# First pass on a 512-column ramp: three strips begin with four row tiles, both K strips take six of the later ten first, the other scale and shift columns come in between

## The chip, the cores and the metric

The kernel runs on 1 core of a Trainium2 chip. Its time is the device time of that core in microseconds; the kernel before is given as the median of three runs. TensorE (PE) has a clock that the chip grants at one of two levels, 1.2 or 2.4 GHz; the profile prints the granted share.

## The reference

One decoder layer in float32 on 256 tokens of width 2048: an mLSTM mixer and a gated MLP with a causal convolution, each behind an RMS norm that is modulated by a conditioning vector `c`.

```python
def modulation(c, w_mod, b_mod):
    m = jax.nn.silu(c) @ w_mod + b_mod
    return jnp.split(m[:, None, :], 6, axis=-1)
...
        sh1, sc1, g1, sh2, sc2, g2 = modulation(c, *mod_params[layer])
        hm = rms_norm(x) * (1.0 + sc1) + sh1
        if layer % N_MIXERS == 0:
            y = mlstm_mixer(hm, l0_w_in, l0_gate_bias, l0_h_norm, l0_w_out)
...
        x = x + g1 * y
        hf = rms_norm(x) * (1.0 + sc2) + sh2
        x = x + g2 * conv_ffn(hf, *ffn_params[layer])
```

`mlstm_mixer` begins with `proj = h @ w_in`, whose 6144 wide columns are the queries, keys (K), values (V) and output gates (O), and 16 small gate columns. The change touches only the first modulation (`sc1`, `sh1`: each 2048 columns of `w_mod`, 16.8 MB) and the product `h @ w_in`.

## The kernel before

**Staging of the product.** The product is cut into 12 strips of 512 columns (four V, four O, two K, two Q) and the 2048 rows of `w_in` into 16 row tiles of 128. A unit of work is a half: two row tiles of one strip, 512 KB, 12 matmuls of 512 columns. A half arrives in one of eight places of `raw`; ScalarE (ACT) rounds it to `w_hi` (`split_hi`), VectorE (DVE) makes the rest `w_lo` (`split_lo`, one 128x1024 subtract, counted by `raw_done`), and PE multiplies both with the modulated tokens `hm_hi`, `hm_lo`. `w_hi` and `w_lo` have four places. DVE's and ACT's loops over `p` split half `p + 3` while PE works on half `p`; ACT first waits until PE has done `p` halves. In the text p is the number of a half in PE's order and half v is the same count for loads.

**Two passes.** The first pass (p = 0 to 35) takes the first six row tiles of all 12 strips, three halves each. The second pass (p from 36, `V_PASS1`) takes the other ten row tiles, five halves each, the K strips first. A strip's partial sums lie in two PSUM banks; ACT stores them when the strip is done (`store_strip`) and puts them back for the second pass.

**Why two passes.** A row tile of tokens can be modulated only when its 128 columns of scale and shift are known, and each of those is a sum over all 2048 rows of `w_mod`. The first 768 columns come first: 16 loads `m0` of 768 KB, added on DVE (`add_m0`) and summed on PE (`sum_m0`, `add_first_sums`, with `keep_clock` matmuls between). This stretch is the ramp; PE's first half follows it. The other 1280 columns are added while PE works on the first pass: 32 loads `m1` of 640 KB with one 128x1280 add each (`add_m1`). Their sums are turned by PE (`later_sums`, `turn_rows`), copied by ACT, and the last ten row tiles are modulated at the border of the passes.

**The order of loads.** SyncE (SP) issues all these loads in one order written out by hand, one `m1` load ahead of each half:

```python
            for i in range(2 * KT - 2):
                load_m1(i)
                load_half(6 + i)
...
                    sp.wait_ge(m1_used, i - 5)
...
                    sp.wait_ge(raw_done, RAW0 + vh - 8 + 1)
```

So half v is issued when half v - 8 has been split and the `m1` load before it has its place, one of six. SP waits at an issue that has no place yet, and everything behind it in the order waits too. After the first modulation, 48 loads of 1 MB (`load_mod`, `MOD_LOAD`, `MOD_SLOT`) bring the gate and the second modulation during the second pass and the output projection.

Of the kernel before, what the change touches and what calls it, by code (L numbers as in the profile page):

```python
# [5 lines left out]
def hybrid_mlstm_convffn_adaln_kernel(nc, x_d, c_d, w_mod, b_mod, w_in, gate_bias, h_norm, w_out,  # L6
# [3 lines left out]
    ALU = mybir.AluOpType  # L10
# [57 lines left out]
    M0_COLS, M1_COLS = K_FIRST * P, (KT - K_FIRST) * P  # L68
    WIDE = (85, 128)
# [3 lines left out]
    MOD_SLOT = [V_PASS1 + p for p in (5, 7, 8, 10, 12, 13, 15, 17, 18)] \  # L73
# [11 lines left out]
    MOD_LOAD = [V_PASS1 + 5, V_PASS1 + 6] + [max(V_PASS1 + 6, p + 11) for p in MOD_SLOT[:K_THREE]] \  # L85
# [8 lines left out]
    GROUP = 3 * P  # L94

    GATES_AT = [V_PASS1 + 7 + n for n in range(KT // 2)]
    ROW_KB = (96, 97, 98, 99, 100, 102, 111, 112)
    KQ_TURN = [PAIRS[1] * (s + 1) + 1 for s in range(4)]
    KQ_COPY = [r + 2 for r in KQ_TURN]

    with ExitStack() as ctx:
# [6 lines left out]
        def place(name, shape, offset, dt=f32):  # L108
# [7 lines left out]
        m1 = [place(f"m1_{s}", [P, M1_COLS], (104 if s < 3 else 32) * KB + 4 * M1_COLS * (s % 3))  # L116
              for s in range(6)]
# [63 lines left out]
        sum_rows = [first_rows, first_rows, place("sc2_rows", [P, QUARTER], 189 * KB)]  # L181
# [34 lines left out]
        m1_in = [sem(f"m1_in{s}") for s in range(6)]  # L216
# [151 lines left out]
        def _(sp):  # L368
# [47 lines left out]

            def load_m1(i):
# [7 lines left out]
                col = MOD_ORDER[n] + M0_COLS  # L425
                sp.dma_start(m1[i % 6][:], w_mod[rows:rows + P, col:col + M1_COLS])\
                  .then_inc(m1_in[i % 6], 16)

            def load_half(vh):
# [3 lines left out]
                if vh < 8:  # L433
                    wait_m0((8, 9, 9, 10, 11, 11, 12, 13)[vh])
# [30 lines left out]
            for i in range(2 * KT - 2, 2 * KT):  # L465
                load_m1(i)
            for i in range(2 * KT - 2, 2 * KT):
                load_half(6 + i)
            for vh in range(6 + 2 * KT, V_OUT):
# [65 lines left out]
        def _(pool):  # L535
# [29 lines left out]
            pool.wait_ge(colsum_done, 3)  # L565
            clear_acc(2)
            pool.wait_ge(colsum_done, 4)
            clear_acc(3)
            pool.dma_start(wg_raw[:], w_in[:, COL_G:COL_G + 2 * H].rearrange("(k p) n -> p k n", p=P))\
                .then_inc(wg_in, 16)  # L570
            pool.wait_ge(wg_in, 16)
            for n in range(4):
                for j in range(2):
# [5 lines left out]
                    nc.gpsimd.tensor_tensor(lo, src, hi.bitcast(f32), ALU.subtract).then_inc(wg_made, 1)  # L579

# [58 lines left out]
            pool.wait_ge(colsum_done, 5)  # L639
# [24 lines left out]
        def _(act):  # L664
# [58 lines left out]


# [112 lines left out]
            scale_shift(0, 1, first_sums(0), scale_p[:, 0:K_FIRST], True)  # L837
# [3 lines left out]
            act.wait_ge(xT_copied, K_FIRST // 2)  # L841
            for g in range(K_FIRST // 2):
                modulate_hi(0, 2 * g, 2 * g + 2)
                if g == 0:
                    scale_shift(1, 2, first_sums(1), shift_p[:, 2:K_FIRST], False)
                    act.wait_ge(sc_made, 2)
                if g < 2:
                    split_hi(g + 1)
            act.wait_ge(xT_copied, KT // 2)

            for p in range(V_PASS1):
                wait_from_1(act, half_done, p)
# [1111 lines left out]
```

## Time and profile before

| | |
|---|---|
| median of three runs | 1175.02 us (1174.92 to 1175.26) |
| profiled execution, its own time | 1175.44 us |
| its span | 1173.7 us (1.7 us less than its time) |
| PE busy | 1155.1 us, 98% of the span |
| DVE / ACT / GpSimd busy | 917.8 / 625.8 / 167.7 us |
| first half begins | 44.14 us |
| second pass begins | 146.34 us |

The busy shares are averages over stages. The change lies in the first 175 us: the ramp, where PE waits for loads, and the first pass, where PE hardly pauses. Each row of the trace has a start and a duration in microseconds, the engine, the line, output and inputs, and in brackets how long the engine was idle before it and what released it.

### The profile page before, as it was taken

How to read it: one execution, taken by the hardware profiler on the slowest of the kernel's cores; microseconds unless marked ns; L12 is line 12 of the kernel's file. 1: busy time of each engine (PE TensorE's matmuls, PEld its weight loads, DVE VectorE, ACT ScalarE, POOL GpSimd, SP SyncE). 2: the span in 40 equal slices, each digit the busy share in tenths (PEclk: the TensorE clock that was granted, in tenths of full speed). 3: DMA queues.
4: the chain of work that ended last, by engine and by line, in shares of the span. 5: the costliest groups of instructions: out<-in, count | busy, mean ns of one | idle time of the engine just before them, and what ended most of it. 6: DMA issues, size and time to landing. Idle time of an engine off the chain costs nothing.

```text
span 1173.7 us, 17088 instructions
## 1 busy us (share of the span) xinstructions
PE 1155.1 (98%) x5888; PEld 980.9 (84%) x5888; DVE 917.8 (78%) x998; ACT 625.8 (53%) x911; POOL 167.7 (14%) x171
## 2 busy tenths in 40 slices
PE   5999999999999999999999999999999999999998
PEld 5888788888887888888888888888888788888886
DVE  6899897998989979888885547888885446777766
ACT  4444565666554556555554446555554445555442
POOL 0000140202121321222120001122120001221200
PEclk9999999999999999999999999999999999999999
DMA  9999999999999967988867577788775666666562
GB/s 371 397 401 402 398 364 346 368 406 376 367 383 369 399 184 209 258 222 257 235 217 244 183 230 232 209 260 233 210 235 197 219 194 185 194 193 179 195 197 74
DMA packets 260953, 316.66 MB, mean 270 GB/s; under 512 B 6328, under 2 KB 187264, under 8 KB 251944
## 3 DMA queue, kind: packets, MB, share of 16 engines
q1 hardware_dynamic: 259488, 312.50, 80.0%
q0 software_dynamic: 944, 3.34, 0.8%
q8 instruction: 28, 0.46, 0.2%
q10 hardware_dynamic: 474, 0.21, 0.1%
q14 instruction: 19, 0.16, 0.0%
HBM read 313.90 MB, written 2.12 MB: 269 GB/s over the span
## 4 chain that ended last, share of the span: by engine, by line
PE 95%; DMA 3%; DVE 1%; SPq 1%; POOL 0%; ACT 0%; issue 0%; DVEq 0%
PE ps L1497 27%; PE ps L1503 14%; PE ps L1537 9%; PE ps L1539 9%; PE ps L1538 9%; PE ps L1608 7%; PE ps L1609 7%; PE ps L1611 7%; DMA m<-in_l_w_mod_dram 3%; PE ps L1616 1%; SPq L413 0%; PE ps L1643 0%; POOL small L593 0%; PE ps L1776 0%; PE ps L1733 0%; PE ps L1826 0%
## 5 line engine op out<-in xcount | busy, mean ns | idle before, releaser
L1116 DVE TENSOR_TENSOR w_lo<-raw,w_hi 128x1024 fp32r<-128x1024 f32 x384 | 471.4, 1230 | 156.5 <-ACT w_hi L676 155.4
L676 ACT ACTIVATE w_hi<-raw 128x1024 fp32r<-128x1024 f32 x384 | 406.0, 1058 | 346.6 <-PE ps L1539 152.0
L1497 PE MATMUL ps<-hm,w_hi 128*128 128x512 f32 x1406 | 338.9, 391 | 0.2 <-DVE hm L1401 0.2
L1497 PEld LDWEIGHTS ps<-hm,w_hi 128*128 128x128 f32 x1406 | 257.4, 188 | 49.0 <-DVE hm L1401 0.4
L1503 PEld LDWEIGHTS ps<-hm,w_lo 128*128 128x128 f32 x1408 | 182.7, 191 | 8.2
L1503 PE MATMUL ps<-hm,w_lo 128*128 128x256 f32 x1408 | 185.3, 283 | 0.0
L1608 PE MATMUL ps<-w_hi,hm 128*128 128x512 f32 x380 | 151.9, 400 | 0.4 <-ACT hm L720 0.4
L1609 PE MATMUL ps<-w_lo,hm 128*128 128x512 f32 x380 | 148.3, 390 | 0.0
L1611 PE MATMUL ps<-w_hi,hm 128*128 128x512 f32 x352 | 137.5, 391 | 0.0
L1537 PE MATMUL ps<-w_hi,act_hi 128*128 128x512 f32 x344 | 134.1, 390 | 0.0
L1538 PE MATMUL ps<-w_lo,act_hi 128*128 128x512 f32 x344 | 134.0, 390 | 0.0
L1539 PE MATMUL ps<-w_hi,act_lo 128*128 128x512 f32 x344 | 134.0, 390 | 0.0
L650 POOL TENSOR_TENSOR act_full<-conv_gate,conv_val 128x256 f32<-128x256 f32 x44 | 32.5, 740 | 510.8 <-DVE conv_val L1444 510.8
L1078 ACT ACTIVATE up_sum<-ps 128x256 f32<-128x256 f32 x84 | 32.0, 381 | 106.4 <-PE ps L1497 106.4
L1608 PEld LDWEIGHTS ps<-w_hi,hm 128*128 128x128 f32 x380 | 71.4, 188 | 18.6 <-issue 3.2
L1609 PEld LDWEIGHTS ps<-w_lo,hm 128*128 128x128 f32 x380 | 71.5, 188 | 14.0
L1135 DVE SCALAR_TENSOR_TENSOR acc<-mod_raw,cT,acc 128x2048 f32<-128x2048 f32 x32 | 75.0, 2345 | 6.1 <-DMA mod_raw<-in_l_w_mod_dram 3.5
L1611 PEld LDWEIGHTS ps<-w_hi,hm 128*128 128x128 f32 x352 | 66.1, 188 | 14.2
L1537 PEld LDWEIGHTS ps<-w_hi,act_hi 128*128 128x128 f32 x344 | 64.6, 188 | 14.2 <-issue 0.8
L1539 PEld LDWEIGHTS ps<-w_hi,act_lo 128*128 128x128 f32 x344 | 64.6, 188 | 13.4
L1538 PEld LDWEIGHTS ps<-w_lo,act_hi 128*128 128x128 f32 x344 | 64.6, 188 | 13.3
L654 POOL TENSOR_TENSOR act_lo<-act_full,act_hi 128x256 f32 x44 | 65.4, 1486 | 23.7 <-DVE act_hi L1451 23.7
(199 smaller groups left out, 1114.9 us busy)
## 6 DMA issues: line engine op xcount, KB each, us to landing
raw<-in_l_w_up_dram SPq DMA_DIRECT2D x88, 1024.0 KB, 5.9
raw<-in_l_w_in_dram SPq DMA_DIRECT2D x96, 512.0 KB, 12.2
mod_raw<-in_l_w_mod_dram SPq DMA_DIRECT2D x48, 1024.0 KB, 7.5
raw<-in_l_w_down_dram SPq DMA_DIRECT2D x44, 1024.0 KB, 5.0
m<-in_l_w_mod_dram SPq DMA_DIRECT2D x32, 640.0 KB, 14.3
raw<-in_l_w_out_dram SPq DMA_DIRECT2D x16, 1024.0 KB, 10.2
m<-in_l_w_mod_dram SPq DMA_DIRECT2D x15, 768.0 KB, 13.1
mod_third<-in_l_w_mod_dram SPq DMA_DIRECT2D x8, 1024.0 KB, 8.1
```

The lines of the kernel that those rows point to most:

```text
L654: nc.gpsimd.tensor_tensor(act_lo[:, part], act_full[:, k, :], act_hi[:, part].bitcast(f32), ALU.subtract)\
L676: nc.scalar.activation(w_hi[:, v % 4, :], raw_half(v), ACT.Copy).then_inc(w_hi_made, 1)
L1116: nc.vector.tensor_tensor(w_lo[:, v % 4, :], raw_half(v), w_hi[:, v % 4, :].bitcast(f32), ALU.subtract)\
L1135: nc.vector.scalar_tensor_tensor(out=part, in0=src, scalar=cT[:, ds(tile, 1)], in1=part, op0=ALU.mult, op1=ALU.add).then_inc(mod_done, 1)
L1497: return mm(ps[:, 4 + w % 4, :], w_hi[:, v % 4, j * P:(j + 1) * P], both, start=(k == 0), stop=stop, skip_group_check=True)
L1503: return mm(ps[:, 4 + w % 4, 0:SEQ], w_lo[:, v % 4, j * P:(j + 1) * P], hm_hi[:, k, :], start=False, stop=stop, skip_group_check=True)
L1537: mm(out, s_hi, hi, start=first, stop=False, skip_group_check=True)
L1538: mm(out, s_hi, lo, start=False, stop=False, skip_group_check=True)
L1539: last = mm(out, s_lo, hi, start=False, stop=final, skip_group_check=True)
L1608: mm(out, s_hi, hi, start=(k == 0), stop=False, skip_group_check=True)
L1609: mm(out, s_hi, lo, start=False, stop=False, skip_group_check=True)
L1611: last = mm(out, s_lo, hi, start=False, stop=(k == final), skip_group_check=True)
```

## The change

The ramp's loads are cut to 512 columns of scale and of shift (`M0_COLS`: 16 loads of 512 KB). The first three strips take four row tiles each (p = 0 to 5), then their last two (p = 6 to 8), which need columns 512 to 767: eight new loads `m0b` of 4 x 128 rows by 256 columns, with 32 adds of 256 columns on DVE (`add_m0b`) and the sums `ramp_sums` on PE behind p = 5. The other columns come in two groups: 32 loads of 768 columns and then 32 of 512, in five places in place of six. `m1_due(p)` says how many adds stand behind each split: four to every three halves from p = 6, then three to each half from p = 31 to 41. SP's order follows it: `m1_ahead(vh)` loads are issued before half `vh`. The two K strips of the second pass take row tiles 6 to 11 (p = 36 to 41) and then 12 to 15 (p = 42 to 45). ACT makes the full modulated tile too (`modulate_full`), DVE only subtracts (`low_part`). The loads and adds of the later modulation move three to four halves later.

```diff
-    M0_COLS, M1_COLS = K_FIRST * P, (KT - K_FIRST) * P
-    WIDE = (85, 128)
+    K_RAMP, K_MORE = 4, 12
+    M0_COLS, MB_COLS = K_RAMP * P, (K_FIRST - K_RAMP) * P
+    M1_COLS = ((K_MORE - K_FIRST) * P, (KT - K_MORE) * P)
+    M1_GROUPS = ((3, 2 * P), (4, P))
+    WIDE = (P, P)
+    ORDER = [(m, kp) for m in range(3) for kp in range(2)] + [(m, 2) for m in range(3)] \
+        + [(m, kp) for m in range(3, STRIPS) for kp in range(PAIRS[0])] \
+        + [(STRIPS + m, 3 + kp) for m in range(2) for kp in range(3)] \
+        + [(STRIPS + m, 6 + kp) for m in range(2) for kp in range(2)] \
+        + [(m, kp) for m in range(STRIPS + 2, 2 * STRIPS) for kp in range(3, 8)]
...
-    MOD_LOAD = [V_PASS1 + 5, V_PASS1 + 6] + [max(V_PASS1 + 6, p + 11) for p in MOD_SLOT[:K_THREE]] \
+    MOD_LOAD = [V_PASS1 + 9, V_PASS1 + 9] + [max(V_PASS1 + 9, p + 11) for p in MOD_SLOT[:K_THREE]] \
...
+    ROWS_SUMMED = (18, 31, V_PASS1, V_PASS1 + 5)
+    ROWS_TURNED = (20, 32, V_PASS1 + 2, V_PASS1 + 5)
+    ROWS_COPIED = (19, 32, V_PASS1 + 1, V_PASS1 + 6)
+    SCALES_TAKEN = (21, 33, V_PASS1 + 3, V_PASS1 + 6)
+    MODULATED = (34, 35, V_PASS1, V_PASS1 + 6, V_PASS1 + 7)
...
+        def m1_due(p):
+            if p <= 30:
+                return max(0, min(2 * KT, 4 * (p - 5) // 3))
+            return min(M1_TILES, 2 * KT + 3 * (p - 30))
+
+        def m1_ahead(vh):
+            return min(M1_TILES, m1_due(vh - 5) + 4)
...
+            def load_m0b(i):
+                n, rows = i // 4, 4 * (i % 4) * P
+                if i < 4:
+                    sp.wait_ge(xT_ready, KT // 2)
+                else:
+                    sp.wait_ge(m0b_used, 4 * (i - 3))
...
             def load_m1(i):
-                n, rows = i // KT, (i % KT) * P
-                if i < 3:
+                b, n, rows = i // (2 * KT), i // KT % 2, (i % KT) * P
+                if i < 5:
                     sp.wait_ge(xn_made, TB)
-                elif i < 6:
-                    wait_m0((14, 14, 15)[i - 3])
                 else:
-                    sp.wait_ge(m1_used, i - 5)
+                    sp.wait_ge(m1_used, i - 4)
...
-            for vh in range(6):
+            load_half(0)
+            for vh in range(1, 9):
                 load_half(vh)
-            for i in range(2 * KT - 2):
-                load_m1(i)
-                load_half(6 + i)
+                load_m0b(vh - 1)
+            issued = 0
+            for vh in range(9, V_OUT):
+                while issued < m1_ahead(vh):
+                    load_m1(issued)
+                    issued += 1
                 load_due_mods(vh)
                 load_half(vh)
...
+            def scales_and_shifts(p):
+
+                if p == K_FIRST:
+                    for n, out in ((0, scale_p), (1, shift_p)):
+                        scale_shift(n, 3, ps[:, n, 0:2 * P].rearrange("p (k c) -> p k c", c=P)[:, :, 0],
+                                    out[:, K_RAMP:K_FIRST], n == 0)
+                    act.wait_ge(sc_made, 4)
+                    modulate_hi(0, K_RAMP, K_FIRST)
...
+                if p in MODULATED:
+                    act.wait_ge(sc_made, 6 if p < SCALES_TAKEN[3] else 8)
+                    modulate_later(K_FIRST + 2 * MODULATED.index(p))
...
             for p in range(V_PASS1):
-                if p == V_PASS1 - 1:
-                    dve.wait_ge(sc_made, 6)
-                    modulate_lo(0, K_FIRST, K_FIRST + 2)
+                adds_and_low_parts(p)
                 split_lo(p + 3)
-                if 1 <= p <= 2 * KT:
-                    add_m1(p - 1)
+                for i in range(8):
+                    if (0, 0, 1, 2, 2, 3, 3, 4)[i] == p:
+                        add_m0b(i)
+                for i in range(m1_due(p - 1), m1_due(p)):
+                    add_m1(i)
...
+            def ramp_sums():
+
+                pe.wait_ge(m0b_used, 2 * KT)
+                for n in range(2):
+                    for k in range(2):
+                        c0 = M0_COLS + k * P
+                        last = mm(ps[:, n, k * P:(k + 1) * P], acc[:, n, c0:c0 + P], ones[:], start=True, stop=True)
+                last.then_inc(colsum_done, 1)
```

DVE's order, from the split of half 3 on. Before, a split and one add of 1280 columns take turns (`w_lo` rows are splits, the first pair being those of halves 3 and 4; `acc` rows are adds):

```order
L1116 TENSOR_TENSOR w_lo<-raw,w_hi 128x1024 x2
L1164 SCALAR_TENSOR_TENSOR acc<-m_0_53,cT,acc 128x1280
L1116 TENSOR_TENSOR w_lo<-raw,w_hi 128x1024
L1164 SCALAR_TENSOR_TENSOR acc<-m_1_54,cT,acc 128x1280
L1116 TENSOR_TENSOR w_lo<-raw,w_hi 128x1024
```

In the changed kernel, at the same place (the row ahead of this piece holds the splits of halves 2 and 3; the first split below is that of half 4):

```order
L1215 SCALAR_TENSOR_TENSOR acc<-m0b,cT,acc 128x256 x8
L1165 TENSOR_TENSOR w_lo<-raw,w_hi 128x1024
L1215 SCALAR_TENSOR_TENSOR acc<-m0b,cT,acc 128x256 x4
L1165 TENSOR_TENSOR w_lo<-raw,w_hi 128x1024
L1215 SCALAR_TENSOR_TENSOR acc<-m0b,cT,acc 128x256 x8
L1165 TENSOR_TENSOR w_lo<-raw,w_hi 128x1024
L1215 SCALAR_TENSOR_TENSOR acc<-m0b,cT,acc 128x256 x8
L1165 TENSOR_TENSOR w_lo<-raw,w_hi 128x1024
L1215 SCALAR_TENSOR_TENSOR acc<-m0b,cT,acc 128x256 x4
L1165 TENSOR_TENSOR w_lo<-raw,w_hi 128x1024
L1231 TENSOR_SCALAR hm_full<-hm_full,scale_p,shift_p 128x256
```

The 32 short adds now stand between the splits of halves 3 and 8, and the modulation of row tiles 4 and 5 stands behind them.

SP's order. Before, from the first half on, six halves go first and then one `m` load (1280 columns) and one half in turn:

```order
L439 DMA raw<-in_l_w_in_dram 128x2x512 x6
L426 DMA m_0_53<-in_l_w_mod_dram 128x1280
L439 DMA raw<-in_l_w_in_dram 128x2x512
L426 DMA m_1_54<-in_l_w_mod_dram 128x1280
L439 DMA raw<-in_l_w_in_dram 128x2x512
```

In the changed kernel, behind half 8 and the last `m0b` load:

```order
L460 DMA m_0_53<-in_l_w_mod_dram 128x768
L460 DMA m_1_54<-in_l_w_mod_dram 128x768
L460 DMA m_2_55<-in_l_w_mod_dram 128x768
L460 DMA m_3_56<-in_l_w_mod_dram 128x768
L473 DMA raw<-in_l_w_in_dram 128x2x512 x2
L460 DMA m_4_57<-in_l_w_mod_dram 128x768
L473 DMA raw<-in_l_w_in_dram 128x2x512
L460 DMA m_0_53<-in_l_w_mod_dram 128x768
L473 DMA raw<-in_l_w_in_dram 128x2x512
L460 DMA m_1_54<-in_l_w_mod_dram 128x768
L460 DMA m_2_55<-in_l_w_mod_dram 128x768
L473 DMA raw<-in_l_w_in_dram 128x2x512
```

The last of these is half 13; the `m` load right before it is number 7 (counted from 0), and by `load_m1` it waits for three adds done, the third of which stands behind the split of half 11.

PE's order at the place where the last 512 columns are summed, behind p = 41 (the first two rows end p = 41, the third and fourth are the last sums and their turn):

```order
L1676 MATMUL ps<-w_lo,hm 128x512
L1678 MATMUL ps<-w_hi,hm 128x512
L1710 MATMUL ps<-acc,ones 32x128 x4
L1718 MATMUL ps<-ident,first_rows 128x128
L1675 MATMUL ps<-w_hi,hm 128x512
```

Before, the last such sums stood inside p = 35; they now stand inside the second pass.

## Rows read from the trace of the kernel before

**Rows 1.** The page: chain that ended last, shares of the span by engine

```profile
PE 95%; DMA 3%; DVE 1%; SPq 1%; POOL 0%; ACT 0%; issue 0%; DVEq 0%
```

**Rows 2.** The chain of waits in order of time: start, length, what

```profile
27.25 13.82 DMA m<-in_l_w_mod_dram
```

**Rows 3.** Windows: busy of PE, PEld, DVE, ACT, POOL; granted clock, DMA share, GB/s

```profile
28.00:30.00 2.00, 2.00 (x11) 2.00 (x11) 1.55 (x2) 0.18 (x1) 0.00 (x0) 0.50 1.02 398
30.00:40.00 10.00, 8.89 (x56) 7.74 (x56) 7.24 (x8) 0.00 (x0) 0.00 (x0) 0.96 1.03 399
60.00:80.00 20.00, 20.00 (x90) 16.58 (x89) 19.68 (x16) 9.69 (x12) 0.00 (x0) 1.00 1.04 401
160.00:400.00 240.00, 239.90 (x1111) 197.01 (x1111) 212.75 (x186) 140.21 (x233) 49.93 (x52) 1.00 0.99 375
```

**Rows 4.** Timeline of PE in the ramp, and its first half

```profile
17.54 5.16 PE L1675 MATMUL ps<-ident,xn 128*128 128x128 f32 x32
...
22.54 2.81 PE L1692 MATMUL ps<-c_wide,m 128*128 128x85 f32 x24
...
28.60 2.61 PE L1692 MATMUL ps<-c_wide,m 128*128 128x128 f32 x12
31.04 1.46 PE L1665 MATMUL ps<-still 128*128 128x256 f32 x6
32.34 1.50 PE L1692 MATMUL ps<-c_wide,m 128*128 128x128 f32 x12
...
42.22 1.61 PE L1702 MATMUL ps<-ones,acc 128*128 128x128 f32 x12
...
44.14 1.17 PE L1577 MATMUL ps<-w_hi,hm 128*128 128x512 f32 x4
```

**Rows 5.** Timeline of DVE: first work behind the ramp; split of half 2

```profile
42.97 0.16 DVE L1196 COPY shift_p<-ps 128x2 f32<-128x2 f32 x1 [0.80 <-PE ps L1702]
...
48.51 1.22 DVE L1116 TENSOR_TENSOR w_lo<-raw,w_hi 128x1024 fp32r<-128x1024 f32 x1
```

**Rows 6.** Groups on DVE by shape: busy us, mean ns

```profile
L1164 DVE SCALAR_TENSOR_TENSOR acc<-m,cT,acc 128x1280 f32<-128x1280 f32 x32 | 49.6, 1550 | 5.5 <-DMA m<-in_l_w_mod_dram 5.5
L1155 DVE SCALAR_TENSOR_TENSOR acc<-m,cT,acc 128x768 f32<-128x768 f32 x23 | 23.4, 1018 | 9.7 <-DMA m<-in_l_w_mod_dram 8.7
L1439 DVE SCALAR_TENSOR_TENSOR conv_gate<-up_sum,cvT,conv_gate 128x255 f32<-128x255 f32 x44 | 21.4, 487 | 0.0
```

**Rows 7.** Timeline of DVE in the ramp: three adds in one row

```profile
12.76 3.19 DVE L1155 SCALAR_TENSOR_TENSOR acc<-m,cT,acc 128x768 f32<-128x768 f32 x3 [0.86 <-DMA m<-in_l_w_mod_dram]
```

**Rows 8.** Timeline of PE: start of half 6, of the second pass, around half 43

```profile
60.91 0.39 PE L1608 MATMUL ps<-w_hi,hm 128*128 128x512 f32 x1
...
146.34 0.47 PE L1608 MATMUL ps<-w_hi,hm 128*128 128x512 f32 x1 [0.36 <-ACT hm L720]
...
166.18 1.04 PE L1629 MATMUL ps<-ident,kq 128*128 128x128 f32 x8
166.97 0.48 PE L1608 MATMUL ps<-w_hi,hm 128*128 128x512 f32 x1
...
169.81 0.62 PE L1733 MATMUL ps<-hm,wg 128*104 128x512 f32 x2
170.26 0.39 PE L1608 MATMUL ps<-w_hi,hm 128*128 128x512 f32 x1
```

**Rows 9.** Loads: size each, median us from issue to landing; 0 to 50 us

```profile
raw<-in_l_w_in_dram SPq DMA_DIRECT2D x10, 512.0 KB, 12.3
```

**Rows 10.** The same at the kernel's end, and the DMA's busy tenths there

```profile
DMA  8179049418803793960799920000000053004050
...
raw<-in_l_w_down_dram SPq DMA_DIRECT2D x6, 1024.0 KB, 5.0
```

**Rows 11.** Timeline of ACT at the border of the passes

```profile
145.59 1.09 ACT L720 ACTIVATE hm<-hm_full,shift_p,scale_p 128x256 fp32r<-128x256 f32 x2
146.59 1.04 ACT L676 ACTIVATE w_hi<-raw 128x1024 fp32r<-128x1024 f32 x1
```

More of the change, by code:

```diff
@@ L115, in hybrid_mlstm_convffn_adaln_kernel @@
         m0 = place("m0", [P, 8, 2 * M0_COLS], 0)
-        m1 = [place(f"m1_{s}", [P, M1_COLS], (104 if s < 3 else 32) * KB + 4 * M1_COLS * (s % 3))
-              for s in range(6)]
+        m1 = [place(f"m1_{s}", [P, M1_COLS[0]], 104 * KB + 4 * M1_COLS[0] * s) for s in range(5)]
+        m0b = place("m0b", [P, 4, 4 * MB_COLS], 152 * KB)
         w_hi = place("w_hi", [P, 4, HALF], 48 * KB, f32r)
@@ L215, in hybrid_mlstm_convffn_adaln_kernel @@
         m0_used, m0_summed = sem("m0_used"), sem("m0_summed")
-        m1_in = [sem(f"m1_in{s}") for s in range(6)]
+        m0b_in = [sem(f"m0b_in{s}") for s in range(4)]
+        m0b_used = sem("m0b_used")
+        m1_in = [sem(f"m1_in{s}") for s in range(5)]
         m1_used = sem("m1_used")
@@ L638, in _ @@
                 add_y(i)
-            pool.wait_ge(colsum_done, 5)
+            pool.wait_ge(colsum_done, 8)
             clear_acc(5)
@@ L722, in modulate_hi, with modulate_full @@
                              .then_inc(hm_hi_made, 1)
+            def modulate_full(first, last):
+                for k in range(first, last):
+                    nc.scalar.activation(xnT[:, k, :], xnT[:, k, :], ACT.Identity,
+                                         bias=shift_p[:, k:k + 1], scale=scale_p[:, k:k + 1])\
+                             .then_inc(hm_scaled, 1)
             nc.scalar.preload_act_table(ACT.Silu)
@@ L1157, in add_m0, with add_m0b @@
                                                    op0=ALU.mult, op1=ALU.add).then_inc(m0_used, 1)
+            def add_m0b(i):
+                n = i // 4
+                part = acc[:, n, M0_COLS:M0_COLS + MB_COLS]
+                dve.wait_ge(m0b_in[i % 4], 16 * (n + 1))
+                for j in range(4):
+                    rt = 4 * (i % 4) + j
+                    wait_from_1(dve, m0b_used, 4 * i + j)
+                    nc.vector.scalar_tensor_tensor(out=part, in0=m0b[:, i % 4, j * MB_COLS:(j + 1) * MB_COLS],
+                                                   scalar=cT[:, rt:rt + 1], in1=part,
+                                                   op0=ALU.mult, op1=ALU.add).then_inc(m0b_used, 1)
             def add_m1(i):
-                n = i // KT
-                dve.wait_ge(m1_in[i % 6], 16 * (i // 6 + 1))
+                b, n = i // (2 * KT), i // KT % 2
+                dve.wait_ge(m1_in[i % 5], 16 * (i // 5 + 1))
                 wait_from_1(dve, m1_used, i)
-                part = acc[:, n, M0_COLS:D]
-                nc.vector.scalar_tensor_tensor(out=part, in0=m1[i % 6][:],
+                part = acc[:, n, M1_FROM[b] * P:M1_FROM[b] * P + M1_COLS[b]]
+                nc.vector.scalar_tensor_tensor(out=part, in0=m1[i % 5][:, 0:M1_COLS[b]],
                                                scalar=cT[:, i % KT:i % KT + 1], in1=part,
@@ L1586, in in_half @@
                 first, final = (0, 2 * PAIRS[0] - 1) if n == 0 else (2 * PAIRS[0], KT - 1)
-                if 2 * kp == first and m >= 2:
+                if 2 * kp == first and m >= 3:
                     if n == 0:
@@ L1690, in sum_m0 @@
                 pe.wait_ge(m0_in[i % 8], 16 * (n + 1))
-                for k in range(K_FIRST):
+                for k in range(K_RAMP):
                     last = mm(first_sum(n, k), m0[:, i % 8, k * P:(k + 1) * P],
@@ L1700, in add_first_sums @@
                 pe.wait_ge(m0_used, m0_added(8 * n + 7)[0])
-                for k in range(K_FIRST):
+                for k in range(K_RAMP):
                     last = mm(first_sum(n, k),
```

199 lines of the change are left out of this document (104 added, 95 removed).

## The prediction, made before the changed kernel ran

> **What bounds the kernel now.** The chain that ended last is PE for 95% and DMA for 3% [rows 1]. The DMA part is the ramp: in the chain of waits, 13.8 us up to 41.07 are loads of `w_mod` alone [rows 2], and the queue moves 399 GB/s at a DMA share above 1 [rows 3]. PE begins its first half at 44.14 [rows 4], and half 6, 36 and 44 (after 166.18 and 169.81, a batch of transposes and of gate sums) at 60.91, 146.34 and 170.26 [rows 8]: 2.80 us a half up to half 6, of which 12 matmuls at a pitch near 0.227 are 2.73. In the first pass three engines are nearly level: DVE is busy 19.68 of 20 us, DMA moves 401 GB/s [rows 3]; a half and its `m1` load are 1.18 MB, 2.93 us. From 160 to 400 us PE is busy 239.9 of 240 [rows 3]. So what is lost before half 44 is lost at the end: PE has nothing there to run faster with.
>
> All sums below are differences of PE's clock times at the start of a half, made against the profiled time, 1175.44 us, 0.42 above the median.
>
> **The ramp, -6.9.** The loads shrink from 12.6 to 8.4 MB: 4.19 MB at 400 GB/s are 10.5 us. PE's own chain allows less. It ends the transposes at 22.70 (17.54 + 5.16) and cannot begin the sums of load 4 before; they were 24 matmuls in 2.81, then 12 in 1.50, with a row of six still matmuls in 1.46 [rows 4]. Now: 16 matmuls at 0.117 (1.9), the first sums (8 at 0.17, 1.3), five batches of 8 at 0.125 (5.0) and three still rows (4.4): the last sums begin at 35.3, where they began at 42.22 [rows 4], 6.9 earlier. So PE's half 0 starts at 37.2 and DVE's copy at 36.1 in place of 42.97 [rows 5]. (One batch took 2.61 in place of 1.50 where the granted clock was 0.50 [rows 3, 4]; should that come again, 0.5 less is gained.) DMA is in time: its last ramp load lands near 31 to 33, with a gap of up to 2 us since load 12 waits for the sums behind the transposes. A cheaper load gives no more than 6.9.
>
> **The short adds, +15.0.** Behind the ramp DVE must make, before the sums of columns 512 to 767: its opening work up to the split of half 2, 5.5 us (48.51 - 42.97) [rows 5]; the splits of halves 2 to 7 (6 x 1.22 = 7.3); and 32 adds of 256 columns. No such add is in the trace on this tile. The 1280 and 768 column adds took 1.550 and 1.018, 1.04 ns a column with 0.22 fixed, so 0.49 for 256; the convolution's 255 columns took 0.487 [rows 6]. Adds that depend on each other follow at 0.066 more ((3.19 - 1.02) / 2 - 1.02) [rows 7]. So 32 x 0.56 = 17.9. Bounds: 0.26 (columns alone, 8.4 in all) and 0.6. From 36.1: 36.1 + 5.5 + 7.3 + 17.9 = 66.8. Then the sums (8 matmuls, 1.0), two copies and waits (0.6), one modulation (0.55, half of 1.09 [rows 11]): half 6 starts at 69.0. PE alone would be there at 37.2 + 16.8 = 54.0. 69.0 - 60.91 = 8.1 late, where the ramp had made it 6.9 early: +15.0. Nothing hides this: PE stands at the sums, and all its other halves are behind them.
>
> The Trainium skill (VectorE: DVE Perf Modes, "The TRN2 errata — SBUF-src ops pay a fixed extra latency per instruction") gives a float32 two-input add of N columns (N + 151)/0.96 ns, 0.42 us for 256, and warns against many small tiles, which speaks against this change. The row above is 0.06 us longer than the page's figure for its 255 columns; by the page this term would be 2 us less.
>
> **The loads' distance, +10.4.** Before, half v is issued when half v - 8 is split, and lands 12.3 us later, behind 5 MB of others [rows 9]. Now the load ahead of it must have its place. By the order, half 16 is issued after the first add behind the split of half 14 and is itself split two splits later. So landings come round in a loop. A lone load of 1 MB lands in 5.0 us at the end, where the DMA is idle between loads [rows 10]; 1 MB at 401 GB/s is 2.6, so 2.3 to 2.4 is fixed. Half 16 then lands 4.1 us after its issue (part of a 384 KB load ahead, 1.31 of its own, 2.3 fixed). From there: rounding 1.06 [rows 11], split 1.22, add 1.02, split 1.22, add 1.02, five semaphores at 0.07 and one issue 0.4: 10.3 us to the issue of half 19. That is 3.43 a half, where PE needs 2.73, the transfers 2.62 (3.15 MB to three halves) and DVE's own work 2.6. 27 halves (9 to 35) take 92.6, less the two halves (5.5) that DVE is ahead at half 9: 87.1, before 77.2 (146.34 - 69.1, half 9 being three halves behind 60.91). +9.9, and 0.5 for waits on the fresh row tiles at half 6. Bounds: 0 if the landings were always in time, +14 with 0.4 us more on each of the nine loops.
>
> The Trainium skill (DMA: Bandwidth & Descriptors, "Anatomy of one DMA — SWDGE (gpsimd) path") puts a load's fixed cost at about 2.0 us. Here the row gives 2.4 for SP's queue; by the page's figure this term and the next would together be some 5 us smaller.
>
> **The K strips, +27.0.** From p = 31 three adds of 512 columns (0.76 each) go with each split. Half v + 2 is issued after the second add behind the split of v: 3.7 to land, 1.06, 1.22, 1.52, 0.3 for semaphores, 0.4 for the issue: 8.2 for two halves, 4.1 each. Half 36 starts at 146.34 + 8.1 + 10.4 = 164.8, when its split is done. Eight splits on, half 44 is split at 197.6 and the 64th add is done at 199.2. Only then can PE sum (behind p = 41), ACT copy, PE turn, ACT take the scale and modulate: 1.9. Half 42 starts at 201.1 and ends at 204.6 with the wait for its second tile. Half 43 needs row tiles 14 and 15, which ACT modulates behind the rounding of half 45. SP issues half 45 behind two 1 MB loads, which wait for the 64th add too: issued 200.1, landed 209.2 (5.2 + 1.3 + 2.4 and 0.2), rounded and modulated 211.0. Half 44 starts at 214.5. Before: 170.26, with 0.79 of transposes and 0.45 of gate sums done that are still to come: 214.5 - 170.26 + 1.25 = 45.5, and 45.5 - 18.5 = 27.0. Bounds: 16 (landings in time; then DVE's 11 halves of 3.5 to 3.9 and the chain behind the last add remain) and 33 (0.4 us more on each of five landings, and PE restarting at the lower clock).
>
> The sum is -6.9 + 15.0 + 10.4 + 27.0 = +45.5: 1175.44 + 45.5 = 1220.9, against the median 1220.5. What is moved at no price: the later loads of 1 MB (PE-bound stretch, DMA at 375 of 401 GB/s), `modulate_full` on ACT (busy 140 of 240 us [rows 3]), the stores of strips 0 to 2, each due 2.7 us after the strip's end and 2.1 long. If that cover were gone, PE would wait under 1 us at half 9.
>
> **Rivals.**
> *Landings in time.* If the fixed part of a landing overlaps with what is in flight, the two loops vanish and engine work alone is left: -6.9 + 15.0 + 0.5 + 16 = +24.6, 1200. For it: before, DVE waited for `m1` loads only 5.5 us in all [rows 6]. Against it: then 5 MB were in flight; now SP may not issue. Chance 0.15.
> *A slower clock besides.* After idle stretches PE ran a batch in 2.61 in place of 1.50, at the granted 0.50, the 1.2 GHz level [rows 3, 4]. Waits of 5 to 14 us stand ahead of halves 6, 37, 42 and 43; each restart would cost 1.5 to 3.4, of which those ahead of 42 and 43 reach the end. With 0.3 us more on each landing: 1220.5 + 6 + 5, 1231. Chance 0.15.
> *Faster: a short add costs its columns alone.* At 0.26 the adds end at 57.3 and half 6 starts at 59.5, 1.4 early; the sign at that place turns at 0.31 an add (36.1 + 12.8 + 32x + 2.2 = 60.9). With later landings in time and DVE's saved time hiding the K strips' adds, 1173.6. Against it, 255 columns at 0.487 [rows 6]. Chance 0.03.
> *No change*, the ramp's gain met by a wait of the same size: 0.02.
> The forecast has 0.65, and for itself 1210 to 1230.
>
> **The numbers.** 0.2% (2.3 us) is about what a measurement can tell from no change here. All cases but the last two are slower by more: slower 0.95, same 0.02, faster 0.03. The range reaches from the first rival to the second: 1199 to 1233 leaves out some 0.1 below and 0.07 above.
>
> **What the changed profile would show.** Half 0 at 36 to 37.5; DVE's rows of 256 columns near 0.49 each and without idle time up to 66; PE idle for 10 to 14 us ahead of the sums behind p = 5, released by DVE; a DMA share clearly below 1 between 45 and 200 us; ACT's `w_hi` waiting for `raw` all through the first pass; PE waits of 5 us and more for `acc` or `hm` between 165 and 215. The forecast is wrong if PE's wait ahead of half 6 is under 5 us, if halves 9 to 35 keep 2.8 us each, or if the DMA share stays at 1.

## The result and the profile after

The changed kernel takes 1247.51 us (median of 4 runs, 1244.67 to 1248.86) against 1175.08 us (4 runs, 1174.92 to 1175.26): a ratio of 1.0613, 95% interval 1.060 to 1.0626. Forecast were 1220.5 us and 1199 to 1233: slower was right, the size was 27 us short.

The page of the changed kernel: chain that ended last [rows 1].

```profile
PE 74%; DMA 13%; DVE 7%; issue 3%; ACT 2%; SPq 1%; POOL 0%; DVEq 0%; ACTq 0%
```

Its windows, columns as in [rows 3]:

```profile
60.00:70.00 10.00, 2.78 (x10) 2.42 (x11) 7.54 (x14) 1.68 (x5) 0.00 (x0) 0.57 0.82 312
...
100.00:120.00 20.00, 11.14 (x47) 7.59 (x48) 13.77 (x14) 7.62 (x10) 0.00 (x0) 0.81 0.74 237
180.00:200.00 20.00, 10.43 (x35) 7.21 (x35) 16.45 (x24) 10.54 (x17) 0.00 (x0) 0.57 0.84 261
200.00:220.00 20.00, 10.11 (x45) 7.95 (x44) 12.90 (x16) 4.41 (x5) 2.35 (x2) 0.87 0.91 304
...
260.00:280.00 20.00, 15.09 (x63) 12.07 (x63) 14.78 (x12) 7.85 (x11) 0.00 (x0) 0.91 0.83 297
```

PE, DVE and DMA, nearly level before, all have gaps now: in 100 to 120 us none of them is busy for more than 0.74 of the time. This stretch is bound by a loop of waits, not by an engine. PE's timeline at the places of [rows 4] and [rows 8]; the starts of halves 0, 6, 36 and 44 are 37.32, 69.30, 179.30 and 232.50 (12 matmuls of 512 columns to a half, counted from the first):

```profile
37.32 1.17 PE L1648 MATMUL ps<-w_hi,hm 128*128 128x512 f32 x4 [0.38 <-ACT hm L751]
...
66.11 2.08 PE L1736 MATMUL ps<-ones,acc 128*128 128x128 f32 x8 [8.17 <-DVE acc L1215]
...
69.30 0.76 PE L1675 MATMUL ps<-w_hi,hm 128*128 128x512 f32 x1 [1.11 <-ACT hm L751]
...
179.30 0.47 PE L1675 MATMUL ps<-w_hi,hm 128*128 128x512 f32 x1 [2.03 <-DVE w_lo L1165]
...
193.82 0.65 PE L1710 MATMUL ps<-acc,ones 128*32 128x128 f32 x8 [8.08 <-DVE acc L1224]
...
220.38 0.65 PE L1710 MATMUL ps<-acc,ones 128*32 128x128 f32 x8 [10.26 <-DVE acc L1224]
...
232.50 0.40 PE L1675 MATMUL ps<-w_hi,hm 128*128 128x512 f32 x1
...
261.82 0.50 PE L1675 MATMUL ps<-w_hi,hm 128*128 128x512 f32 x1 [1.73 <-DVE w_lo L1165]
...
268.92 0.50 PE L1675 MATMUL ps<-w_hi,hm 128*128 128x512 f32 x1 [3.18 <-DVE w_lo L1165]
```

The two waits from 260 on were not in the forecast. They follow from DVE (e2 below tries it), which waits four times for 1 MB modulation loads in the second pass (timeline):

```profile
245.67 2.35 DVE L1184 SCALAR_TENSOR_TENSOR acc<-mod_raw,cT,acc 128x2048 f32<-128x2048 f32 x1 [3.85 <-DMA mod_raw<-in_l_w_mod_dram]
251.99 2.35 DVE L1184 SCALAR_TENSOR_TENSOR acc<-mod_raw,cT,acc 128x2048 f32<-128x2048 f32 x1 [2.83 <-DMA mod_raw<-in_l_w_mod_dram]
258.28 2.35 DVE L1184 SCALAR_TENSOR_TENSOR acc<-mod_raw,cT,acc 128x2048 f32<-128x2048 f32 x1 [2.80 <-DMA mod_raw<-in_l_w_mod_dram]
265.37 2.35 DVE L1184 SCALAR_TENSOR_TENSOR acc<-mod_raw,cT,acc 128x2048 f32<-128x2048 f32 x1 [3.61 <-DMA mod_raw<-in_l_w_mod_dram]
```

One turn of the loads' loop, on three queues. SP issues half 16 and, a turn later, half 19:

```profile
92.59 0.43 SPq L473 DMA_DIRECT2D raw<-in_l_w_in_dram  x1
...
105.36 0.43 SPq L473 DMA_DIRECT2D raw<-in_l_w_in_dram  x1
```

ACT rounds halves 16, 17, 18 and 19, each as soon as it lands:

```profile
97.89 1.06 ACT L707 ACTIVATE w_hi<-raw 128x1024 fp32r<-128x1024 f32 x1 [4.65 <-DMA raw<-in_l_w_in_dram]
101.71 1.06 ACT L707 ACTIVATE w_hi<-raw 128x1024 fp32r<-128x1024 f32 x1 [2.76 <-DMA raw<-in_l_w_in_dram]
103.86 1.06 ACT L707 ACTIVATE w_hi<-raw 128x1024 fp32r<-128x1024 f32 x1 [1.08 <-DMA raw<-in_l_w_in_dram]
...
110.87 1.06 ACT L707 ACTIVATE w_hi<-raw 128x1024 fp32r<-128x1024 f32 x1 [4.99 <-DMA raw<-in_l_w_in_dram]
```

From issue to rounding are 5.30 us (92.59 to 97.89), then 5.51 (105.36 to 110.87); forecast were 4.1. The leading splits of the turns (halves 19, 22, 25, 28, 31) stand at 111.96, 123.50, 135.20, 146.43 and 158.04: 11.5 us a turn, not 10.3. (The first turn, 98.98 to 111.96, took 13.0: there DVE also waited for half 17, rounded only at 101.71.)

### The profile page after: what moved, and what is told of

Same layout as the page of the kernel before. It is cut to its first block, busy times and chain, and to the rows that moved or that the text cites. A ratio compares the mean times of both kernels' runs of the same rounds, so it can differ in the third digit from the quotient of the medians.

```text
span 1247.1 us, 17194 instructions
## 1 busy us (share of the span) xinstructions
PE 1172.0 (94%) x5868; PEld 986.7 (79%) x5868; DVE 931.2 (75%) x1052; ACT 632.8 (51%) x925; POOL 161.6 (13%) x171
## 4 chain that ended last, share of the span: by engine, by line
PE 74%; DMA 13%; DVE 7%; issue 3%; ACT 2%; SPq 1%; POOL 0%; DVEq 0%; ACTq 0%
PE ps L1568 26%; PE ps L1574 13%; PE ps L1608 8%; PE ps L1610 8%; PE ps L1609 8%; DMA raw<-in_l_w_in_dram 7%; PE ps L1675 2%; PE ps L1676 2%; DMA m<-in_l_w_mod_dram 2%; DMA mod_raw<-in_l_w_mod_dram 2%; DMA mod_third<-in_l_w_mod_dram 2%; DVE acc L1224 2%; PE ps L1678 2%; DVE acc L1184 2%; ACT w_hi L707 1%
## 5 line engine op out<-in xcount | busy, mean ns | idle before, releaser
L1675 PE MATMUL ps<-w_hi,hm 128*128 128x512 f32 x380 | 159.5, 420 | 18.3 <-DVE w_lo L1165 15.5
L1676 PE MATMUL ps<-w_lo,hm 128*128 128x512 f32 x380 | 154.3, 406 | 0.0
L1678 PE MATMUL ps<-w_hi,hm 128*128 128x512 f32 x352 | 140.5, 399 | 0.0
L1675 PEld LDWEIGHTS ps<-w_hi,hm 128*128 128x128 f32 x380 | 75.3, 198 | 42.1 <-DVE w_lo L1165 16.3
L1184 DVE SCALAR_TENSOR_TENSOR acc<-mod_raw,cT,acc 128x2048 f32<-128x2048 f32 x32 | 76.1, 2380 | 16.9 <-DMA mod_raw<-in_l_w_mod_dram 13.4
L1676 PEld LDWEIGHTS ps<-w_lo,hm 128*128 128x128 f32 x380 | 75.3, 198 | 15.3
L1678 PEld LDWEIGHTS ps<-w_hi,hm 128*128 128x128 f32 x352 | 67.9, 193 | 15.1
## 6 DMA issues: line engine op xcount, KB each, us to landing
raw<-in_l_w_out_dram SPq DMA_DIRECT2D x16, 1024.0 KB, 10.3
```

The costliest lines, as they stand in the source:

```text
L1184: nc.vector.scalar_tensor_tensor(out=part, in0=src, scalar=cT[:, ds(tile, 1)], in1=part, op0=ALU.mult, op1=ALU.add).then_inc(mod_done, 1)
L1675: mm(out, s_hi, hi, start=(k == 0), stop=False, skip_group_check=True)
L1676: mm(out, s_hi, lo, start=False, stop=False, skip_group_check=True)
L1678: last = mm(out, s_lo, hi, start=False, stop=(k == final), skip_group_check=True)
```

## The experiments

Theory A, from the trace: after half 12 the loads' distance sets the pace, and the forecast's loop was right but its time from issue to use too short. Rival B: DVE's work and the bytes set it. Times are medians of 4 runs of each kernel; the kernel before had 1175.1 to 1176.1 in the same groups.

**e1_halves_7_ahead**

```diff
-            return min(M1_TILES, m1_due(vh - 5) + 4)
+            return min(M1_TILES, m1_due(vh - 7) + 4)
```

> The m1 loads are issued two halves later in SP's order, so that a half's load goes out up to seven halves ahead of its use instead of five; all else as in the changed kernel. Theory A (distance): after half 12 a half's load is held behind an m1 load whose place comes free five halves before, and with 5.3 us from the issue to its rounding three halves take 11.8 us. Then three halves fall to about 8.6 us, half 36 starts at 154 to 156 us (179.3 in the changed kernel), half 44 at 198 to 204 us (232.7), and the time is 28 to 33 us lower, about 1217 us. Rival B (work): DVE's adds and the bytes of more, narrower row tiles set the pace whatever the order; then half 36 moves by less than 3 us and the time stays at 1244 to 1248 us.

1216.47 us, 31.0 less. Half 36 starts at 155.33 and half 44 at 202.59. Its window, where all three engines are level again:

```profile
100.00:120.00 20.00, 20.00 (x95) 15.94 (x94) 16.95 (x16) 9.61 (x14) 0.00 (x0) 1.00 1.01 366
```

Halves 9 to 35 take 75.6 us (79.74 to 155.33), 2.80 each, where the changed kernel takes 99.1 (80.25 to 179.30), and nothing of DVE's work or of the bytes was taken away. B falls for them. Ahead of the last adds a new wait appears, since two 1 MB loads now go out before the last `m1` loads (DVE's timeline):

```profile
187.06 1.61 DVE L1224 SCALAR_TENSOR_TENSOR acc<-m,cT,acc 128x512 f32<-128x512 f32 x2 [6.32 <-DMA m<-in_l_w_mod_dram]
```

**e10_halves_6_ahead**, the same line with `vh - 6`.

> The changed kernel with a half's load going out up to six halves ahead (five in it, seven in the first run). Theory A (the loop is the time from a load's issue to its use, shared by the halves it is ahead): one half more takes most of it, half 36 starts at 156 to 160 us and the time is 1219 to 1223 us. Rival B (a threshold of order, so that each half ahead gives the same again): about half of the 31 us, 1230 to 1233 us.

1223.71 us, 23.8 less (0.7 us above A's bound); half 36 at 156.51. One half more takes nearly all of the loop's wait, as A has it: half 36 is only 1.2 us behind the seven-ahead kernel's. In the traces the seventh half brings 2.7 us more in the K strips.

**e14_no_early_m1_loads**

```diff
             def load_m1(i):
...
+                if 5 <= i < 2 * KT:
+                    return
                 col = MOD_ORDER[n] + M1_FROM[b] * P
```

(The adds' waits are set so that they ask only for loads that are issued.)

> Leaves out part of the computation: the changed kernel, order of loads and all waits as they are, without issuing m1 loads 5 to 31 (their adds work on what lies in the places), so that the halves 12 to 35 travel almost alone. It measures the term that was mis-sized: a half's time from issue to rounding, 5.3 us in the changed kernel, forecast at 4.1 from lone loads. Theory A (the forecast held for a lone half, the rest is m1 traffic in the same queue): 3.9 to 4.4 us, three halves in 9 to 10.3 us, half 36 starts at 158 to 166 us (179.3) and the time falls by 13 to 21 us. Rival B (a lone half of 512 KB takes 5 us or more by itself): half 36 at 174 us or later, less than 6 us.

1232.96 us, 14.6 less; half 36 at 163.35 (forecast for the changed kernel: 164.8). Halves 16, 19, 22, 25 and 28 were rounded 3.8 to 4.1 us after their issue, and their turns took 9.2 to 9.7 us. Half 16, issue and rounding:

```profile
88.71 31.65 SPq L475 DMA_DIRECT2D raw<-in_l_w_in_dram  x12
...
92.56 1.06 ACT L709 ACTIVATE w_hi<-raw 128x1024 fp32r<-128x1024 f32 x1 [3.27 <-DMA raw<-in_l_w_in_dram]
```

The loads in 85 to 150 us, with the DMA's tenths:

```profile
DMA  5007992028990049980079950179900399896069
...
raw<-in_l_w_in_dram SPq DMA_DIRECT2D x20, 512.0 KB, 4.4
```

This is the disputed term nearly by itself: a half that travels alone takes what was forecast. The 1.2 to 1.6 us more are the `m1` loads in the same queue, which the forecast's 4.1 counted only as a part of one. That half 36 comes so near to 164.8 is in part luck: half 9 starts at 78.65 (77.2 by the forecast), and the turns are shorter than the forecast's 10.3, with no `m1` load issued ahead of a half.

**e2_mods_earlier**

```diff
-    MOD_LOAD = [V_PASS1 + 9, V_PASS1 + 9] + [max(V_PASS1 + 9, p + 11) for p in MOD_SLOT[:K_THREE]] \
+    MOD_LOAD = [V_PASS1 + 9, V_PASS1 + 9] + [V_PASS1 + p for p in (16, 17, 18, 18, 19, 20)] \
```

> The six early loads of the gate's modulation tiles (numbers 2 to 7) are issued ahead of halves 52, 53, 54, 54, 55 and 56 instead of 55 to 60; the DVE adds stay where they are. Theory A: DVE's waits for these loads (13.4 us in five between 245 and 272 us) make TensorE late by about 5 us there (1.7 and 3.2 us), and these are carried to the end: the waits fall below 4 us and the time falls by 4 to 9 us, to about 1241 us. Rival B: TensorE is bound by something else by then (the raw ring of six halves), or the late adds only move to a later wait: the time stays within 2 us of 1247.5.

1238.90 us, 8.6 less. In DVE's groups the wait for these loads falls from 13.4 to 2.8 us:

```profile
L1184 DVE SCALAR_TENSOR_TENSOR acc<-mod_raw,cT,acc 128x2048 f32<-128x2048 f32 x32 | 76.2, 2380 | 7.0 <-issue 4.2 <-DMA mod_raw<-in_l_w_mod_dram 2.8
```

From half 44 to the transposes of `a_row` PE takes 49.4 us in place of 55.5 (47.0 before). So the unforeseen term is real: 6 us up to there.

**e4_ahead_and_mods**, both edits.

> Both edits of the first two runs of this group. Theory A for both: their gains add, 32 to 42 us, the time is about 1211 us. Rival: with the halves farther ahead the loads of the modulation tiles are no longer late by themselves and the second edit brings under 2 us, so that the time equals that of the seven-ahead kernel.

1212.97 us: 3.5 less than the seven-ahead kernel, 34.5 less than the changed one, where the two alone sum to 39.6. In the traces the second edit brings from half 44 to the transposes of `a_row` about what it brought alone (48.5 us in place of 54.4), so why the medians do not add in full is not shown. What stays in both is the pair of 1 MB loads in front of the last `m1` loads: DVE still waits 6.88 us for them here.

**e5_pair_behind**, as that, and

```diff
-    MOD_LOAD = [V_PASS1 + 9, V_PASS1 + 9] + [V_PASS1 + p for p in (16, 17, 18, 18, 19, 20)] \
+    MOD_LOAD = [V_PASS1 + 11, V_PASS1 + 11] + [V_PASS1 + p for p in (16, 17, 18, 18, 19, 20)] \
```

> The kernel of both edits of the group before (halves seven ahead, six modulation loads earlier) with the first pair of modulation loads, 2 MB, issued ahead of half 47 in place of 45, so that all 64 m1 loads go out first. Theory A: in the seven-ahead kernels DVE stood 6.3 us for the last m1 loads, which lay behind this pair in the queue, and TensorE stood for DVE; that wait goes and the time falls by 4 to 7 us, to about 1207 us. Rival B: the pair is late in its own turn (its first add is in half 44's place) and the gain is given back there: within 2 us of 1213.

1206.02 us, 7.0 less, and half 44 at 196.89 (202.47). PE's timeline: the third and fourth later sums, and half 42.

```profile
164.20 0.66 PE L1710 MATMUL ps<-acc,ones 128*32 128x128 f32 x8 [6.97 <-DVE acc L1224]
...
185.04 0.42 PE L1710 MATMUL ps<-acc,ones 128*32 128x128 f32 x8 [4.28 <-DVE acc L1224]
...
187.34 0.77 PE L1675 MATMUL ps<-w_hi,hm 128*128 128x512 f32 x1 [0.99 <-ACT hm L751]
```

The next three ask what holds these sums. **e6_narrow_late_adds**, on the pair-behind kernel:

```diff
-                part = acc[:, n, M1_FROM[b] * P:M1_FROM[b] * P + M1_COLS[b]]
+                cols = (M1_COLS[0], 64)[b]
+                part = acc[:, n, M1_FROM[b] * P:M1_FROM[b] * P + cols]
```

> As the pair-behind kernel, and leaves out part of the computation: the 32 later m1 adds work on 64 columns in place of 512 (about 0.30 us each in place of 0.76), their loads stay whole. Theory A (DVE's work bounds the first two K strips, at 4.2 us a half with three such adds and one split): a half takes about 3.3 us there, and the time is 7 to 11 us below the pair-behind kernel. Rival B (the loads bound them, 1.31 MB a half at some 0.4 MB/us are 3.3 us, and the waits for whole column sums do the rest): under 3 us.

1203.45 us (1202.2 to 1204.19), 2.6 less than the pair-behind kernel (1205.09 to 1207.41): B's number. **e7_no_late_m1_loads**, on the same kernel:

```diff
             def load_m1(i):
...
+                if b:
+                    return
```

(The adds' waits are set to the last loads that are issued.)

> As the pair-behind kernel, and leaves out part of the computation: the 32 later m1 loads (256 KB each, 8.4 MB) are not issued, their adds run at full width on what lies in the places. Theory A (DVE's work): the halves of the K strips keep their 4.2 us, and the time is within 4 us of the pair-behind kernel. Rival B (loads): the time falls by more than 8 us.

1205.57 us (1202.87 to 1208.51), no clear difference: A's number. So each run, read alone, clears one of the two and points at the other. The narrow adds take DVE's work from 34.3 to 21.2 us in 145 to 185 us, and its groups there show what it waits for instead:

```profile
L1225 DVE SCALAR_TENSOR_TENSOR acc<-m,cT,acc 128x64 f32<-128x64 f32 x30 | 8.5, 282 | 13.0 <-DMA m<-in_l_w_mod_dram 12.5
```

and without the loads DVE has its full work and no such wait:

```profile
L1226 DVE SCALAR_TENSOR_TENSOR acc<-m,cT,acc 128x512 f32<-128x512 f32 x31 | 23.2, 749 | 2.2
```

**e9_neither_late_adds_nor_loads**, both edits.

> As the pair-behind kernel, and leaves out part of the computation: both the late m1 loads are not issued and their 32 adds work on 64 columns. Alone the two brought 2.6 and 0.5 us. Theory A (DVE's 4.2 us and the loads' 3.8 us a half each take over when the other is gone): together they free the K strips, the third later sums start at 158 us or before (164.2 in the pair-behind kernel), the fourth at 174 to 177 us (185.0), and the time falls by 8 to 12 us. Rival B (the chain of sums, row copy, turns, scale, modulation and split, the same whatever the adds cost, holds them): less than 4 us.

1193.02 us, 13.0 less (A had 8 to 12), where the two alone bring 2.6 and nothing clear. The fourth later sums start at 174.97 (185.04), the third at 160.29 (A had 158 or before). From the split of half 38 to that of half 43 a half takes 3.96 us in the pair-behind kernel, 3.95 without the loads, 3.76 with narrow adds and 2.90 with both. DVE's own work is 3.5 us a half, 4.2 where it also makes the low parts of two row tiles. DVE's work and the loads are nearly level in the K strips, and each hides the other: a pair of such runs says "not this one" twice, and only the third says what it is.

**e3_quarter_short_adds**, on the changed kernel:

```diff
             def add_m0b(i):
...
-                for j in range(4):
+                for j in range(1):
...
-                                                   op0=ALU.mult, op1=ALU.add).then_inc(m0b_used, 1)
+                                                   op0=ALU.mult, op1=ALU.add).then_inc(m0b_used, 4)
```

> Leaves out part of the computation: of each m0b tile's four 256-column adds only the first is done (8 in place of 32), the loads stay. Theory A (the 0.52 us each of the short adds is what holds half 6): 24 adds less are 12.5 us of DVE, of which about 9 us show before another wait takes over; half 6 starts at about 60 to 61 us (69.3), and since the loop behind is a latency loop that starts earlier by as much, half 36 comes 8 to 9 us earlier, at 170 to 171 us, and the time is 8 to 9 us lower, about 1239 us. Rival B: the loads, queued behind each other, set half 6 or half 36, and the time falls by less than 4 us.

1238.49 us, 9.0 less, but not where A put it: half 6 starts at 63.33, 6.0 earlier, not 9. The loads of these columns take over (DVE's timeline):

```profile
56.75 0.49 DVE L1215 SCALAR_TENSOR_TENSOR acc<-m0b,cT,acc 128x256 f32<-128x256 f32 x1 [2.11 <-DMA m0b<-in_l_w_mod_dram]
```

Half 44 is 5.7 earlier. In the traces another 0.7 us comes up to the transposes of `a_row` and 2.5 behind them; this edit does not explain them.

**e8_clock_kept**, on the pair-behind kernel:

```diff
+                keep_clock(24, 0)
                 pe.wait_ge(m0b_used, 2 * KT)
...
+                if s > 1:
+                    keep_clock(14, 0)
                 pe.wait_ge(m1_used, (s + 1) * KT)
```

> As the pair-behind kernel, with matmuls on constants into a free bank ahead of TensorE's three long waits: 24 of 256 columns ahead of the ramp's second sums, 14 ahead of the third and of the fourth later sums. Theory A (the granted clock, 0.69 in 60 to 80 us and 0.66 to 0.83 in 160 to 200 us, costs time of its own behind each wait): the clock there is 0.9 or more and the time falls by 3 to 6 us. Rival B: DVE and the loads set the pace behind these waits, and TensorE's slower matmuls are hidden: the time falls by less than 2 us.

1204.04 us (1202.46 to 1204.56), 2.0 less, on the border between the two theories, and the fastest kernel with the change in it that leaves nothing out. **e12_clock_kept_alone**, on the changed kernel, with 24 in place of 14.

> The changed kernel with only the matmuls on constants put in: 24 of 256 columns ahead of the ramp's second sums, and 24 ahead of the third and of the fourth later sums. Theory A (the low granted clock is a result of the waits and costs little of its own, since the loads' loop sets the pace up to half 44): 1243 to 1247 us, the clock 0.9 or more in 60 to 80 us. Rival B (the clock is a cause beside the loop): 1239 us or less.

1243.06 us (1240.31 to 1246.42), 4.5 less; the ranges of the two kernels overlap. Their windows, the changed kernel first:

```profile
60.00:80.00 20.00, 12.78 (x43) 10.40 (x44) 13.82 (x22) 6.35 (x11) 0.00 (x0) 0.66 0.60 211
...
60.00:80.00 20.00, 18.89 (x89) 15.95 (x88) 16.64 (x24) 9.45 (x15) 0.00 (x0) 1.00 0.66 230
```

Half 9 starts at 77.36 in place of 80.25, half 36 at 175.40 in place of 179.30, half 44 at 230.01 in place of 232.50. So keeping the clock brings 2 to 5 us in all, and up to half 44 what it brings comes from the wait ahead of half 6. The lower clock is a result of the waits first.

**e11_all_left_out**: the edits of e5, e6, e7, e3 and e8 together.

> Leaves out part of the computation: as the clock-kept kernel, with 24 of the 32 short adds left out, the late m1 loads not issued and the late adds on 64 columns. It closes the account of what is left of the change. Theory A: the parts add, 9 us for the short adds and 8 to 12 us for the K strips from 1204, so 1183 to 1188 us, and what is then left over the kernel before (1175) is the serial chain ahead of the last four row tiles, less the ramp's gain. Rival B: something outside of these places was also made slower, and the time stays above 1192 us.

1199.36 us, 6 more than the kernel without two of its edits. That is B's number and, by the next run, not B's reason: the matmuls on constants cost time themselves. Each is two instructions in PE's timeline (48 for 24), and with the waits shorter they hold up what stands behind them:

```profile
53.69 10.52 PE L1758 MATMUL ps<-still 128*128 128x256 f32 x48
...
152.79 6.21 PE L1758 MATMUL ps<-still 128*128 128x256 f32 x28
```

**e13_late_and_short_out** repeats it without them.

> Leaves out part of the computation: the kernel with neither late m1 loads nor full late adds, and also 24 of the 32 short adds left out; without the matmuls on constants, of which each wrote two instructions, 10.5 us in place of the 5 reckoned, so that the run that had them and left everything out paid for them itself. Theory A: the parts add, 9 us less than 1193.0, that is 1183 to 1186 us. Rival B: with the short adds out the later halves wait for something else, and it stays at 1189 us or more.

1188.31 us, 11.0 less than the run before and 4.7 less than with the short adds in: neither theory's number. Half 6 is 5.1 earlier (63.48, from 68.57), and so is half 44 (179.83, from 184.83). The short adds are worth 5 to 6 us until their loads hold half 6; the 9 us of e3 were the wrong size to carry over.

## Why the prediction was right in sign and wrong in size

The starts of PE's halves against [rows 4, 8] give each term. The spans differ by 73.4 us (1247.1 and 1173.7). The profiled run of the changed kernel is the slowest of its four, 1.3 us above the median, and half 0 starts between 36.1 and 37.7 us in the runs, none of which changes the ramp; so a term is good to about 1 us.

- **Ramp, forecast -6.9: -6.8.** Half 0 at 37.32 (forecast 37.2, [rows 4]: 44.14), DVE's copy at 36.10 as forecast.
- **Short adds, +15.0: +15.2.** Half 6 at 69.30 (forecast 69.0, before 60.91). The 256-column add took 0.484 us, forecast 0.49. The cause was only half named: with 24 of 32 adds out, loads hold half 6 at 63.33.
- **The loads' distance, +10.4: +24.6.** This step failed. Half 36 started at 179.30, forecast 164.8. Halves 9 to 35 took 99.1 us, forecast 87.1, and that is 12 of the 14 us missed. The failed sentence is that a half lands 4.1 us after its issue. It was worked out from a load with the DMA idle around it [rows 10], with part of one 384 KB load ahead; here 1.57 MB of `m1` loads go with every 1.57 MB of halves. Measured 5.3 to 5.7 us; alone, in e14, 3.8 to 4.1, and half 36 at 163.35. The loop itself, its order and its other parts were right: nine turns of 1.2 to 1.6 us more are the 12. The bound of "0.4 us more on each of the nine loops" was too tight by three times. The other 2 us are halves 6 to 8, which PE did at the lower clock behind its wait: 10.95 us, before 8.15; in e12, with the clock kept, 8.28. The main sum had nothing for it.
- **K strips, +27.0: +30.5** (half 44 at 232.50; 62.2 late, 1.25 of work still to come, less 33.0 up to half 36). Right within its bounds, but by luck, since two errors had opposite signs. The loads took 4.9 to 5.9 us from issue to rounding in place of 3.7, so that the 64th add ended 41.0 us behind the start of half 36 and not 34.4. From there to half 44 it took 12.2 us and not 15.3. The forecast let the two 1 MB loads wait for the 64th add and half 45 behind them. The change takes that wait out, and SP issued the pair 9 us ahead of the end of that add (218.72 + 1.60); half 45 held half 43 for only 0.78 us:

```profile
210.87 0.82 SPq L420 DMA_DIRECT2D mod_raw<-in_l_w_mod_dram  x2
...
218.72 1.60 DVE L1224 SCALAR_TENSOR_TENSOR acc<-m,cT,acc 128x512 f32<-128x512 f32 x2
```

- **Behind half 44, forecast 0: +10.9**, less 1.0 at the end. "What is moved at no price: the later loads of 1 MB" failed. The change puts the first adds of these tiles on six halves in a row (44 to 49) where they had gaps (they move by 3, 2, 2, 1, 0 and 0 halves, not all by three to four as the text ahead of the prediction has it), while each load still stands in SP's order 11 halves behind the add that frees its place. DMA's mean rate could not show that; each load's issue set against its own add would have. 7.2 us are lost by `a_row` (DVE's four waits; e2 brings 6.1 of them back), 3.7 behind it: there PE waits 1.84 us for `gated` once, which it never did before. That wait stands in the trace of every run with the change in it, with 1.0 to 3.3 us, whatever else was taken out. What makes it was not tried and stays open.
- **Rivals.** Landings in time (0.15): false, they were later. A slower clock besides (0.15): its clock was there (0.57 in 60 to 70 and 180 to 200 us) and keeping it brings 2 to 5 us by e8 and e12, of the 6 it was given. It was given them ahead of halves 42 and 43, where e12 shows none; its "0.3 us more on each landing" should have been 1.2 to 1.6. The faster rival needed an add below 0.31 us: 0.484.
- **The Trainium skill.** VectorE: DVE Perf Modes ("The TRN2 errata — SBUF-src ops pay a fixed extra latency per instruction") makes the 256-column add 0.42 us, an estimate by its formula; measured 0.484. DMA: Bandwidth & Descriptors ("Anatomy of one DMA — SWDGE (gpsimd) path") gives about 2.0 us fixed; e14's 3.8 us less 1.31 for the bytes leave 2.5 for SP's queue with its semaphore. In both the trace's own row was nearer.

What is left over the kernel before in e13 is 13 us (12.9 by the medians of its group). By PE's starts 2.6 us stand at half 6, 3.4 at half 36, 10.8 at half 44 with the work still to come and 11.7 at `a_row`. So most of it, 7.5 us, arises in the K strips, where the chain of sums, copy, turns, modulation and split ahead of halves 37 and 42 is left. Its parts were not separated.

## What to carry to other kernels

Where one queue issues two kinds of loads in a written order, a load waits for the places of the other kind too: count how many uses ahead each is issued, and multiply the number of turns by the time from issue to use with the other kind's traffic in the queue, never by that of a lone load. When uses are moved together, check each load's issue against its own use. Removing one of two level resources shows little (2.6 us and nothing clear here, 13.0 for both); remove both before calling neither the cause.

## What the runs showed of the hardware

Where the loads' rows were narrower, the DMA moved less at nearly the same busy share. Windows of the pair-behind kernel, at shares of 1.01 and 0.93 to 0.97; the loads are of 768-column rows (3 KB) and 2 KB rows up to 131 us, then of 2 KB rows alone:

```profile
80.00:140.00 60.00, 60.00 (x272) 49.05 (x271) 53.48 (x51) 30.58 (x41) 0.00 (x0) 1.00 1.01 365
140.00:150.00 10.00, 10.00 (x51) 7.66 (x50) 7.06 (x9) 5.84 (x10) 0.00 (x0) 1.00 0.93 304
...
160.00:170.00 10.00, 5.80 (x22) 4.37 (x23) 8.86 (x12) 2.02 (x5) 0.00 (x0) 0.66 0.97 311
```

Before, with rows of 5 KB and 2 KB, it was 401 GB/s at 1.04 [rows 3]. In e7, with the halves' 2 KB rows alone and gaps between them, it was 155 GB/s at 0.51 in 145 to 185 us, 304 for a full share. So the K strips' 1.31 MB a half are about 4.2 us at the 311 GB/s shown (an estimate), where 3.3 were reckoned. These are mixed streams: that the width of the rows is the cause is not shown, and why it should cost this was not tried.
